# Finer copy waits, keys first and a column-grouped sample output tile in a hybrid attention step

## What is computed

```python
h = rmsnorm(x, norm_g) * (1 + scale) + shift            # modulation
q, kc, vc, ks, vs, kw, vw, gates, hc, bc, cc, z = split(h @ w_in)
# sample attention: compressed blocks pick the blocks, then selected and window attention
o = g0 * attend(q, k_cmp, v_cmp) + g1 * attend(q, k_sel, v_sel) + g2 * attend(q, k_win, v_win)
# output, prompt and sample alike
y = x + gate * (concat([o * silu(z_a), y_conv * silu(z_c)]) @ w_out)     # 2048 -> 1024
out = rmsnorm(y, final_g)                                # mean of squares over the 1024 columns
```

## Time and profile before

| | us |
|---|---|
| median of 3 runs | 1705.54 |
| profiled execution, its own time | 1708.85 |
| its span, first to last instruction | 1707.0 |
| PE busy | 1543.1 (90%) |
| DVE / ACT / POOL busy | 753.7 / 633.1 / 317.9 |

### The profile page before, as it was taken

One profiled execution on the slowest core, in us unless ns is written; L12 is line 12 of the kernel. 1 busy time (PEld: TensorE's weight loads), 2 busy tenths in 40 slices (PEclk: granted clock), 3 DMA queues, 4 the chain that ended last, 5 costly groups with the idle time before them and its releaser, 6 DMA issues.

```text
span 1707.0 us, 24838 instructions
## 1 busy us (share of the span) xinstructions
PE 1543.1 (90%) x9808; PEld 1321.0 (77%) x9808; DVE 753.7 (44%) x1849; ACT 633.1 (37%) x1255; POOL 317.9 (19%) x379
## 2 busy tenths in 40 slices
PE   4997999999999999699769989989989987899995
PEld 1887999999999999677657757757757755688882
DVE  2541132312313223245477767767767753533321
ACT  2320111111111111145567767757757754521110
POOL 1104000000000000200024434435435430000000
PEclk8998999999999999889969989989989999899998
DMA  9708433232232222385200210110110059553310
GB/s 338 121 26 297 112 76 88 58 92 75 65 97 63 75 75 62 115 280 180 64 31 26 66 38 26 38 38 26 29 47 26 19 215 254 167 169 99 99 59 19
DMA packets 164220, 164.37 MB, mean 96 GB/s; under 512 B 48484, under 2 KB 145252, under 8 KB 158792
## 3 DMA queue, kind: packets, MB, share of 16 engines
q1 hardware_dynamic: 150104, 96.40, 21.1%
q0 software_dynamic: 14000, 66.38, 11.5%
...
## 4 chain that ended last, share of the span: by engine, by line
PE 80%; DVE 5%; ACT 5%; DMA 5%; issue 3%; SPq 0%; POOL 0%; DVEq 0%; ACTq 0%
PE PS L921 32%; PE PS L1242 12%; PE PS L1062 9%; PE PS L1045 6%; PE PS L1022 5%; PE PS L969 4%; PE PS L1023 3%; ACT pr L1393 2%; DMA wor<-in_w_out 2%; DMA wr<-in_w_in 2%; PE PS L883 1%; PE PS L884 1%; PE PS L885 1%; DMA adaw<-in_ada_w 1%; ACT ptt L1413 1%
## 5 line engine op out<-in xcount | busy, mean ns | idle before, releaser
L921 PE MATMUL PS<-hhi,wh 128*128 128x352 f32 x1152 | 251.5, 326 | 8.7 <-issue 8.1
L921 PE MATMUL PS<-hhi,wl 128*128 128x352 f32 x1152 | 249.2, 324 | 0.0
L921 PE MATMUL PS<-hlo,wh 128*128 128x352 f32 x1152 | 248.9, 324 | 0.0
L774 POOL TENSOR_SCALAR pr<-pr,rg 128x640 f32<-128x640 f32 (+7 forms) x128 | 203.9, 1604 | 210.4 <-DVE rg L1753 210.4
L1393 ACT ACTIVATE pr<-PS,nm 128x640 f32<-128x640 f32 (+7 forms) x256 | 178.8, 699 | 77.1 <-DVE nm L1732 74.6
L921 PEld LDWEIGHTS PS<-hhi,wh 128*128 128x128 f32 x1152 | 196.4, 190 | 12.6 <-issue 11.1
L921 PEld LDWEIGHTS PS<-hhi,wl 128*128 128x128 f32 x1152 | 198.6, 188 | 0.0
L921 PEld LDWEIGHTS PS<-hlo,wh 128*128 128x128 f32 x1152 | 196.4, 188 | 0.0
L1045 PE MATMUL PS<-ident,pr 128*128 128x128 f32 x1056 | 148.1, 275 | 8.8 <-ACT pr L1404 5.3
L1605 DVE TENSOR_TENSOR wl<-wr,wh 128x1024 fp32r<-128x1024 f32 x48 | 58.6, 1221 | 187.6 <-ACT wh L1309 187.1
L1062 PE MATMUL PS<-ptt,kvt 128*64 128x256 f32 x1056 | 138.8, 406 | 0.0
...
## 6 DMA issues: line engine op xcount, KB each, us to landing
...
wr<-in_w_in SPq DMA_DIRECT2D x32, 256.0 KB, 3.7
qb<-q_stacked SPq DMA_DIRECT2D x32, 256.0 KB, 3.1
...
```

The source lines that it names most:

```text
L774: ins = po.tensor_scalar(pr[r][:, h, 0:k], pr[r][:, h, 0:k], rg[:, r, h:h + 1], None, ALU.mult)
L921: ins = pe.matmul(PS[:, bank + c, 0:CH], a[kind % 2][:, k, :], b[:, k, c * CH:(c + 1) * CH], start=(k == 0 and b is hhi and a is wh), stop ...
```

## The change

1. `pair_scores` waits per chunk c for the copies of the two groups that this chunk reads. `pair_values` takes the short piece first and then waits in five places, before steps 1, 5, 9, 13 and 17, each time for one copy. `turn_rows` and its copies turn the short pieces first.
2. SP loads window keys 5 and 6 and window values 4 and 5 ahead of the blocks of `w_out`; `early` becomes none, 0 to 2, 3 to 6, 7 to 15.
3. The sample tile is made as 16 blocks, two weight parts and four column groups: each of the four groups has a quarter (256) of the output columns and writes its own 32 partitions of one bank, in fp32 from `mr` itself, 128 matmuls. `mh` and `ml` are not made for it. The result lies folded, 128 partitions of 256 elements; gate, final_g and x are loaded in that layout (`gate4`, `final4`, `x4`), a matmul with a constant 0/1 matrix `fold` adds the four partial sums of squares, and four DMAs store the tile, two from SP and two from POOL.

```diff
@@ early, loads of SP
-            return (range(0, 2), range(2, 4), range(4, 7), range(7, 16))[pq]
+            return (range(0), range(0, 3), range(3, 7), range(7, 16))[pq]
...
-            for j in range(2):
-                load_wo(j)
             load_kw(5)
             load_kw(6)
-            for j in range(2, 7):
-                load_wo(j)
             load_vw(4)
             load_vw(5)
+            for j in range(3):
+                load_wo(j)
             load_kw(7)
+            for j in range(3, 7):
+                load_wo(j)
...
+            sp.dma_start(fold[:, :], k_fold).then_inc(c6_ld, 16)
+            for g in range(4):
+                own = slice(32 * g, 32 * g + 32)
+                sp.dma_start(gate4[own, :], flat(gbd, D + 256 * g, [(D, NB), (0, TS), (1, 256)])).then_inc(c6_ld, 16)
+                sp.dma_start(final4[own, :], flat(final_g, 256 * g, [(0, 32), (1, 256)])).then_inc(c6_ld, 16)
+                sp.dma_start(x4[own, :], xs[:, 256 * g:256 * g + 256]).then_inc(c6_ld, 16)
...
-            sp.wait_ge(y_ev, NTT - 1)
-            sp.dma_start(gbc[0:SAMP, :], flat(gbd, D, [(D, NB), (0, TS), (1, D)])).then_inc(c6_ld, 16)
+            sp.wait_ge(y_out, NTT)
+            for g in range(2):
+                sp.dma_start(ysf[:, 256 * g:256 * g + 256], yo[32 * g:32 * g + 32, 0:256]).then_inc(mix5_st, 16)
+            sp.wait_ge(mix5_st, 48)
@@ PE
             def pair_scores(pq):
-                for n in (2, 1):
-                    pe.wait_ge(*copied(gi[0] - n))
                 if pq:
                     pe.wait_ge(s5_ev, pq)
                 for c in range(5):
+                    for b2 in range(2):
+                        pe.wait_ge(*copied(gi[0] - 10 + 5 * b2 + c))
...
                 for q in part:
-                    if q < 5:
-                        group([(P, s[:, a:a + P]) for a in pos[4 * q:4 * q + 4]])
+                    if q:
+                        group([(P, s[:, a:a + P]) for a in pos[4 * q - 4:4 * q]])
                     else:
                         group([(SAMP, s[:, PAST:SEL]), (SAMP, s[:, SEL + WIN:SEL + WN]), (NSB, pn[:, pq, :])])
 
             def pair_values(pq):
-                for n in (2, 1):
-                    pe.wait_ge(*copied(gi[0] - n))
...
-                    ops = [(0, pt5[:, r, half], vb[b % 4][:, r, :]) for r in range(NSEL)]
-                    ops += [(0, pt5[0:SAMP, 20, half], kvs[0:SAMP, C_VS:C_VS + DKV])]
+                    ops = [(0, pt5[0:SAMP, 20, half], kvs[0:SAMP, C_VS:C_VS + DKV])]
+                    ops += [(0, pt5[:, r, half], vb[b % 4][:, r, :]) for r in range(NSEL)]
...
                 for n, both in enumerate(zip(value_ops(0), value_ops(1))):
+                    if n == 0:
+                        pe.wait_ge(*copied(gi[0] - 6))
+                    if n % 4 == 1 and n <= NSEL + 1:
+                        pe.wait_ge(*copied(gi[0] - 5 + n // 4))
...
-            for tt in range(NTT):
+            for tt in range(NTT - 1):
...
+            for a in range(2):
+                pe.wait_ge(mr_ld[a], 16 * NTT)
+            pe.wait_ge(y_ev, NTT - 4)
+            for k in range(16):
+                for b in (woh, wol):
+                    for g in range(4):
+                        ins = pe.matmul(PS[32 * g:32 * g + SAMP, 0, 0:256], mr[:, k, 0:SAMP], f32(b[k][:, 256 * g:256 * g + 256]),
+                                        start=(k == 0 and b is woh), stop=(k == 15 and b is wol))
+            ins.then_inc(y_mm, 2)
+            pe.wait_ge(c6_ld, 16 * 15)
+            pe.wait_ge(y_act, 2 * NTT - 1)
+            pe.wait_ge(y_ev, NTT - 3)
+            pe.matmul(PS[:, 2, 0:1], fold[:, :], s6[:, 0:1], start=True, stop=True).then_inc(y_mm, 1)
@@ ACT and DVE, behind their loops over the eight prompt tiles
+            act.wait_ge(y_sum, NTT)
+            act.wait_ge(y_st, 16 * (NTT - 1))
+            act.activation(yo[:, 0:256], yf[:, 0:256], ACT.Square, accum_out=s6[:, 0:1]).then_inc(y_act, 1)
+            act.wait_ge(y_ms, NTT)
+            act.activation(s6[:, 2:3], s6[:, 1:2], ACT.Sqrt).then_inc(y_act, 1)
...
-            dve.wait_ge(c6_ld, 32)
+            dve.wait_ge(c6_ld, 16 * 15)
...
+            dve.wait_ge(y_mm, 2 * NTT)
+            dve.wait_ge(y_out, NTT - 1)
+            link(dve.tensor_tensor(yf[:, 0:256], PS[:, 0, 0:256], gate4[:, :], ALU.mult))
+            dve.tensor_tensor(yf[:, 0:256], yf[:, 0:256], x4[:, :], ALU.add).then_inc(y_sum, 1)
+            dve.wait_ge(y_mm, 2 * NTT + 1)
+            dve.tensor_scalar(s6[:, 1:2], PS[:, 2, 0:1], 1.0 / D, EPS, ALU.mult, ALU.add).then_inc(y_ms, 1)
+            dve.wait_ge(y_act, 2 * NTT)
+            link(dve.reciprocal(s6[:, 3:4], s6[:, 2:3]))
+            dve.scalar_tensor_tensor(yo[:, 0:256], yf[:, 0:256], s6[:, 3:4], final4[:, :], ALU.mult, ALU.mult).then_inc(y_out, 1)
```

More of the change, by code:

```diff
@@ L282, in build @@
         fgb = sb("fgb", [P, D], cx=c6)
-        sb("apart8", [P, 896], cx=c6)
+        gate4, final4, x4 = (sb(n, [P, 256], cx=c6) for n in ("gate4", "final4", "x4"))
+        fold = sb("fold", [P, P], cx=c6)
         weights(8, c6)
@@ L449, in tokens_at @@
             return slice(S, TOK) if s == 0 else slice((s - 1) * P, s * P)
+        ysf = y_sample.rearrange("b t c -> (b t) c")
         def rows_of(tt):
@@ L825, in _ @@
                 po.wait_ge(kg_ld[q], (48, 48, 32)[q])
-            for tt in range(NTT):
-                n = rows_of(tt)
+            for tt in range(NTT - 1):
                 po.wait_ge(y_out, tt + 1)
-                dst = y_prompt[0, tt * P:tt * P + n, :] if tt < NTT - 1 else y_sample.rearrange("b t c -> (b t) c")
-                po.dma_start(dst, yo[0:n, :]).then_inc(y_st, 16)
-            po.wait_ge(y_st, 16 * NTT)
+                po.dma_start(y_prompt[0, tt * P:tt * P + P, :], yo[:, :]).then_inc(y_st, 16)
+            po.wait_ge(y_out, NTT)
+            for g in range(2, 4):
+                po.dma_start(ysf[:, 256 * g:256 * g + 256], yo[32 * g:32 * g + 32, 0:256]).then_inc(y_st, 16)
+            po.wait_ge(y_st, 16 * (NTT + 1))
         @block.tensor
@@ L1465, in row_copies @@
                         gi[0] += 1
-                    elif q < 5:
-                        copy_group(pt5[:, 4 * q:4 * q + 4, :])
+                    elif q:
+                        copy_group(pt5[:, 4 * q - 4:4 * q, :])
                     else:
@@ L1517, in squares @@
                 act.activation(s6[0:n, 2:3], s6[0:n, 1:2], ACT.Sqrt).then_inc(y_act, 1)
-            for tt in range(NTT):
-                if tt + 1 < NTT:
+            for tt in range(NTT - 1):
+                if tt + 2 < NTT:
                     mix_high(tt + 1, (0, 1) if tt else (1,))
                 squares(tt)
+            act.wait_ge(y_sum, NTT)
[3 more added lines that the diff above has]
+            act.activation(s6[:, 2:3], s6[:, 1:2], ACT.Sqrt).then_inc(y_act, 1)
         @block.vector
@@ L1896, in last_row_copies @@
                     dve.wait_ge(t5, n + 1)
[L1897 to L1900 removed]
+                    dve.tensor_copy(pt5[:, 4 * q - 4:4 * q, :], PS[:, 6 + n % 2, :].rearrange("p (a c) -> p a c", a=4)).then_inc(ev5d, 1)
             def mix_low(tt, halves=(0, 1)):
@@ L1932, in _ @@
                 wo_low(j)
-            dve.wait_ge(c6_ld, 32)
-            for tt in range(NTT):
-                n, b0 = rows_of(tt), 2 * (tt % 4)
-                if tt + 1 < NTT:
+            dve.wait_ge(c6_ld, 16 * 15)
+            for tt in range(NTT - 1):
+                b0 = 2 * (tt % 4)
+                if tt + 2 < NTT:
                     mix_low(tt + 1, (0, 1) if tt else (1,))
```

23 lines of the change are left out of this document (9 added, 14 removed).

## The result

The changed kernel takes 1685.02 us (median of 4 runs, 1676.91 to 1686.46) beside 1705.53 us for the kernel before on the same chip: a ratio of 0.987, 95% interval 0.984 to 0.990. The forecast was 1687.0 us. On another chip, later, the same two kernels had 1687.10 us (10 runs) and 1701.6 us (12 runs; a thirteenth, of 1803.34 us, had a granted clock of 0.833 where the others have 0.960 to 0.969, and is left out), a ratio of 0.993 (0.991 to 0.996). The gain is real in both, 20.5 us in the first comparison and 14.5 us in the second, so its size is known only to some 6 us. The forecast of 18.5 us is a ratio of 0.989: the first interval contains it, the second doesn't. The sections that follow say why.

A forecast was written before the change was run, and what follows sets the result against it. PE bounds the kernel from 1384 us on whenever it isn't waiting. Sample attention 8.6 us plus tail 9.9 us gives 18.5 us off the 1705.54 us median: 1687.0 us, range 1683 to 1693.

The forecast's parts named there:

- Gaps ahead of scores and values: Sample attention: PE's 0.69 to 0.83 us waits for the last copy go; 2.27 us gained up to values 0.
- Keys of pair 2: Sample attention: without weight work on ACT or DVE they take 7.4 us instead of 14.81; gain 7.4 us.
- Sample tile: End of program: 32 steps of four matmuls at 0.45 us, 14.4 us instead of 22.4; gain 8.0 us.
- Chain: Behind the sample tile: products on 128 x 256 elements save 3.0 us, 2.5 net of the fold matmul.
- Tail in all: Sample tile 8.0, chain 2.5, less 0.55 for a second POOL store: gain 9.9 us.
- the load term between values 1 and scores 3: w_out blocks needed 19 us after issue; 4 MB at 273 GB/s land in 15 us, so no wait.
- rival A: Weight work only moves: late blocks or longer PE stops lowering the clock cost 4 to 10 us, 1691 to 1697; chance 0.12.
- ACT waiting for `wor` in pair 1: Sign of a wrong forecast: ACT waits for its weight load in pair 1 of sample attention; no size given.
- a lower clock in 1440 to 1455 us: Sign of a wrong forecast: PE's clock low in this stretch, where it was not low before.
- room below the forecast: Low-clock stretch at 1480 us, around values 3, might be shorter or gone: up to 3.6 us, outside the sum.
- 8.6 in the sum: Sample attention's total gain in us: 9.3 - 1.2 + 0.7 - 0.25.
- a measurement to tell 3.4 us: Claim that measuring this kernel tells some 0.2%, or 3.4 us, from no change.

The follow-up runs named there:

- loads ahead of the cast: Changed kernel with weight blocks 0 to 2 loaded before window values 4 and 5: 1680.38 us, ratio 0.989 to the kernel before.
- the second trace: The changed kernel, unedited, run and profiled once more: 1687.10 us, ratio 0.993 to the kernel before.
- the output part only: Kernel before with only the sample output tile changed (column groups, folded chain, four stores, small loads): 1692.87 us for 1702.97, ratio 0.993.
- the attention part alone: Kernel before with only sample attention changed (waits, loads, where weight blocks are split): 1699.03 us, ratio 0.998.
- the last experiment: Kernel with all 16 blocks split in pair 3, DVE copying pair 3's third and fifth row groups instead of second, fourth, sixth: 1676.84 us, ratio 0.985.
- the version with all blocks late: Changed kernel with all 16 weight blocks split in pair 3, none earlier: 1676.47 us, ratio 0.987; second series 1668.90 us, ratio 0.980.
- the single strip: Changed kernel with all four sample-tile groups in array columns 0 to 31, three quarters of the sample output left out: 1730.49 us, one run.

## Why the prediction was right, and where it was not

**The terms that came out for their own reasons.** Gaps ahead of scores and values: 2.45 us for 2.3 up to values 0, and 3.1 to 3.4 us for four of them when they were put back. Keys of pair 2: 7.1 us long as forecast (7.4). The gain there is 7.85 us against the trace of before and 6.7 against the other trace of the old code, whose stop is 1.2 us shorter. Sample tile: 8.3 for 8.0, its step at the lower bound of the range given (0.432; I had taken 0.45 between the bounds, where the rate of the matmuls in sample attention was the better guide). Chain: 2.5 for 2.5. Tail in all: 10.57 for 9.9, and the same in the experiment.

**The step that failed is the load term between values 1 and scores 3**: "4 MB in 15 us: no wait, with 4 us to spare". ACT asked for block 2 at about 1435.7 (1438.61 - 2.91), some 18 us after SP began to issue it, for the 19 of the sum; but ACT was let go only at 1438.6, 18.7 us after its second half was issued. The rate was as assumed, 268 GB/s from 1414.67 to 1438.61 for 273. The bytes were not: in these 23.94 us that is 6.4 MB, for the 4 MB of the sum. SP had issued window keys 7 and blocks 3 to 6, 2.25 MB, between 1420.6 and 1427.2, and the sum took what is issued behind a load as if it came behind it. That these loads are what delayed it fits the bytes, but was not tested by itself. With the load out of the way the whole step is 2.2 us shorter.

The rest of the miss is the clock. The step has two pieces, in us:

| | forecast | after | loads ahead of the cast |
|---|---|---|---|
| scores 2 to `turn_o` | 18.25 | 20.88 | 18.22 |
| `turn_o` to scores 3 | 5.33 | 6.29 | 6.75 |

The forecast's pieces are those of the earlier trace rows, 17.08 us with a further `wol` of 1.17, and 6.16 us without the 0.83 ahead of the scores. With the load out of the way the first piece is what the sum has, so three casts and three `wol` cost what was forecast and no more, and the 2.6 us lost there are the load's. The second piece was taken at the upper level of the clock, and it runs in a low stretch in both traces: 1.0 and 1.4 us that the sum had at nothing. Together the step lost 3.9 us for 0.3. The two are both ways of rival A, which had a chance of 0.12, with 3.6 us just under its price of 4 to 10; "ACT waiting for `wor` in pair 1" and "a lower clock in 1440 to 1455 us" were named as the marks of a wrong forecast, and both are there. In the second trace, with the stop of 5.07 us, the step from scores 2 to scores 3 takes 28.93 us for 27.17.

**What cancelled it was luck.** In the profiled pair values 3 gained 2.6 us, since the clock came back 3.4 us sooner. I had it as room below the forecast (up to 3.6), not as a term, and it can't be put down to the change: in the second trace of the changed kernel values 3 took 7.89 us (94.39 to 102.28), and with the old attention code in the trace of the output part only 7.17. Without it, the profiled pair would have shown 16.1 us from t0.

**How good the sum is.** By the means of the traces sample attention gained 5.2 us, and by the runs of the attention part alone 3.9, for 8.6 in the sum; the tail gained 10.1 to 10.6 for 9.9. The two parts alone add up to 14.0 us by their medians, and the second comparison of the whole change has 14.5. So the median of the first comparison, 2 us from the forecast, is closer than the mechanism deserves: the sum was right in the tail, and in sample attention some 3 to 5 us too high. The prediction also trusted a measurement to tell 3.4 us, where medians of the same kernel pair differ by 6.

**Stores** cost 0.2 us for 0.55: POOL's second issue took its 0.5 us, but less followed it.

## What to carry to other kernels

Side work that is moved "later" on helper engines still has to sit where the engines it shares have slack. Look for a stage in which PE has a long queue of independent work, as tile 0 had here, and put all of it there, instead of spreading it over stages in which a copy or a combine stands behind it. When a load's landing is worked out as bytes over rate, count what is issued behind it too, as long as it is under way (here 6.4 MB moved where 4 had been counted), and compare with the median time to landing in a stretch that is as full (21.8 and 18.9 us in the two traces here). A removed stop can turn into a new one a stage later, as with the last experiment, so compare by landmarks from a mark ahead of the edit, and follow them up to the end of the program. And take a second trace of either kernel before a landmark's difference is read as the effect of the edit: the same code differed by 2.6 and 3.6 us here.

## What had not been expected

The same code ahead of t0 ends up to 15 us apart: t0 is at 1369.3 to 1370 us in three traces, at 1372 in one and at 1378 to 1384.6 in the others. Two traces of kernels that differ only behind t0, from 600 us to t0:

```profile
600.00:1379.24 779.24, 692.45 (x4703) 561.39 (x4701) 469.47 (x1394) 439.77 (x995) 246.59 (x257) 0.95 0.22 66
```

```profile
600.00:1369.33 769.33, 681.17 (x4704) 557.13 (x4702) 469.17 (x1394) 440.17 (x995) 247.05 (x257) 0.96 0.23 66
```

As many instructions on every engine, DVE and ACT equally busy, but PE busy for 692 us against 681, at a mean granted clock of 0.95 and 0.96. The second series of the version with all blocks late falls in two groups that are about as far apart, three runs at 1666.7 to 1668.9 and two at 1675.6 and 1676.6 us (its first series is more spread out), and the runs of the kernel before reach from 1692.6 to 1709.3. With spreads of this size a median of four runs can carry some 5 us of luck, by my estimate: the first comparison gave 20.5 us and the second 14.5, where the stages from t0, both against the one trace of before, gave 18.75 and 15.2. What makes an execution fall in one group or the other stays open.

Four fp32 column groups of 32 columns cost no more than one group: 0.432 us for a step of four, and 1.73/4 = 0.432 us for one matmul in the single strip, with eight weight-load records a step (0.35 us busy of PEld) beside the matmuls.
